# Four row buffers in place of five in a one-core MLA, sparse attention and PEER block, with reordered first loads and last stores

## The chip, the core and the metric

One core of a Trainium2 chip runs one launch. Its engines work in parallel from their own instruction queues and meet through semaphores: TensorE (PE in the profile, its weight loads PEld), VectorE (DVE), ScalarE (ACT), GpSimd (POOL) and SyncE (SP). DMAs are issued from the queues of SP, ACT and POOL. The metric is the device time of the launch in microseconds (us); the time before is the median of three runs.

## What is computed

A transformer layer for 256 tokens of width 2048 in float32: RMSNorm, an input projection (2048 x 4944), two groups of attention heads side by side, an output projection, a second RMSNorm, and a PEER layer with 16384 single-neuron experts. The part around the change is PEER:

```python
def peer(h, w_pq, sub_keys, u_tab, v_tab):
    def block(hb):
        b, t, _ = hb.shape
        qr = (hb @ w_pq).reshape(b, t, PEER_HEADS, 2, PEER_DKEY // 2)
        sc = jnp.einsum('bthpd,hpnd->bthpn', qr, sub_keys, preferred_element_type=jnp.float32)
        s_top, i_top = lax.top_k(sc, PEER_TOPK)
        cand = s_top[..., 0, :, None] + s_top[..., 1, None, :]
        c_top, c_pos = lax.top_k(cand.reshape(b, t, PEER_HEADS, PEER_TOPK * PEER_TOPK), PEER_TOPK)
        ...
        expert = i0 * PEER_NKEYS + i1
        g = jax.nn.softmax(c_top, axis=-1)
        u = u_tab[expert]
        a = jax.nn.gelu(jnp.einsum('bthkd,btd->bthk', u, hb, preferred_element_type=jnp.float32),
                        approximate=False)
        return jnp.einsum('bthk,bthkd->btd', (g * a).astype(v_tab.dtype), v_tab[expert])
```

Each token picks 8 x 16 = 128 experts. u_tab and v_tab are 134 MB each.

## The kernel before

**Two ways through PEER.** 96 of the 256 tokens ("own" tokens) go by gathers: for each of their picks the rows of u_tab and v_tab are fetched. The other 160 tokens (N_DN) go densely: all 128 units of u_tab (a unit is 128 experts, 1 MB) are multiplied by TensorE with the tokens' activations hF (the U pass, L1525), ScalarE applies GELU (L757), the result is multiplied by a gate matrix, and all 128 units of v_tab are multiplied with it (the V pass, L1580). Every fourth row of the first 128 tokens (`helpers`) lends its place to the picks of the others, so the picks of 96 tokens fill 96 gathers per table in 128 partitions. A gather brings one row of 2048 floats to each of the 128 partitions, 1 MB. There are 192, numbered n = 0 to 191: 96 of u_tab's rows, 96 of v_tab's.

**Row buffers.** Gathers go round through `row`, NROW buffers of 8 KB per partition; row[0] lies among the activations (`acts`), where before the gathers the gain row of the second norm is held, the others lie in `late`, the memory that the split weights and hidden state use until the last w_pq piece. A gather that reuses a buffer waits until VectorE has used it:

```python
                if n >= NROW:
                    pool.wait_ge(row_used, n + 1 - NROW)
                if n >= N_OWN:
                    pool.wait_ge(unit_used, PACE_FROM + (n - N_OWN) * (PACE_TO - PACE_FROM) // N_OWN)
```

The second wait paces V gathers by the units that TensorE has used. All gathers go through POOL's one queue. Ahead of every 16th u gather, POOL copies the lent picks of one head between partitions (`lend_picks`, L485 to L490), a small DMA on the same queue, and waits for it to land before it issues the next gather.

**VectorE** (next_row, L1134 to L1147) takes a u row (L1141: multiply with hs and sum, the dot product) or a v row (L1145: multiply with its weight and add to acc). While the top-k of PEER runs, it takes two rows after each head; in the late U pass it takes one row after each unit, except every 16th, behind its other work there, in program order: the one-hot matrices (hots, L1189) or the gate (L1203), then the multiply of a unit's GELU by ones or gates (apply, L1213), then the row.

**ScalarE** in the late U pass: GELU of unit c (needs the multiply of unit c - 2, whose buffer of two it reuses), in odd units the issue of the load of unit c + 4 (odd_unit, L777), and the scaling of the one-hot matrices for one gate group (hot_scale, L759 to L770). **TensorE** multiplies a unit, then in every second unit the gate group (L1542), which needs that scaling. The ring of units has four buffers; SP issues the even loads.

**Head.** The hidden state is split into a high and a low part as it is made: ScalarE norm_hi (L564, needs xT and the gains) and split_hi of weights (L544), VectorE norm_lo (L834) and split_lo (L821), then TensorE three matmuls for each piece. The first two k-slices of xT and the gains are issued by ScalarE, xT first; the first weight unit is one DMA of 512 KB from SP.

**Tail.** The last v unit closes the eight bank pairs of the output one after the other; ScalarE copies a pair out (L797), TensorE transposes it back (out_transposes, L1570), VectorE adds the residual (L1289), SP stores four groups of columns, two stores each (L426, L427).

## Time and profile before

| | |
|---|---|
| runs before, median (lowest to highest) | 1669.94 us (1669.61 to 1670.95) |
| the profiled execution: its time, its span | 1671.05 us, 1669.3 us |
| TensorE busy | 1656.0 us, 99% |
| VectorE, ScalarE, GpSimd busy | 1020.8, 504.0, 280.1 us |
| DMA, mean over the span; in the U and V passes | 341 GB/s; 392 to 422 GB/s in the page's slices 14 to 39 of 40 |

Busy time counts instructions of the engine, not the issue of DMAs. The page's chain of work that ended last runs for 85% of the span over TensorE and for 9% over DMAs; a DMA in it between about 875 and 1016 us is a gather or a copy of picks.

### The profile page before, as it was taken

The numbers are of one execution on the slowest core, as the hardware profiler recorded it, in microseconds if no ns is written. First come the engines' busy times: TensorE is split into PE (matmuls) and PEld (weight loads), VectorE is DVE, ScalarE is ACT, GpSimd is POOL, SyncE is SP. The second block draws the span as 40 slices with busy tenths as digits, with TensorE's granted clock in tenths as the row PEclk, the third lists the DMA queues.
The fourth block names the chain that finished last, engine by engine and source line by source line (L and its number), as shares of the span: only waits on it lengthen the run. The fifth ranks groups of instructions, "written<-read, shape, count | busy, mean of one in ns | idle before, by whom it ended". The sixth has DMA issues, their size and how long they took to land.

```text
span 1669.3 us, 28850 instructions
## 1 busy us (share of the span) xinstructions
PE 1656.0 (99%) x11438; PEld 1570.3 (94%) x11438; DVE 1020.8 (61%) x1709; ACT 504.0 (30%) x1347; POOL 280.1 (17%) x252
## 2 busy tenths in 40 slices
PE   9999999999999999999999999999999999999999
PEld 7768888888999999999999999999999999999998
DVE  5426695767778999867777767753444333433333
ACT  6547567656551000035444454410000000000000
POOL 1020000000003222312212122222112211221110
PEclk9999999999999999999999999999999999999999
DMA  9674445465648999999999999999999999999996
GB/s 355 226 149 125 139 135 193 139 225 201 224 159 334 421 397 419 411 392 420 395 422 420 421 401 422 422 421 421 421 421 417 417 415 421 422 417 419 421 415 237
DMA packets 107056, 569.90 MB, mean 341 GB/s; under 512 B 11280, under 2 KB 13456, under 8 KB 48208
## 3 DMA queue, kind: packets, MB, share of 16 engines
q1 hardware_dynamic: 56768, 216.22, 34.5%
q0 software_dynamic: 31792, 220.50, 32.9%
q10 hardware_dynamic: 18432, 132.41, 19.2%
q8 instruction: 29, 0.48, 0.1%
q14 instruction: 35, 0.29, 0.0%
HBM read 563.04 MB, written 4.46 MB: 340 GB/s over the span
## 4 chain that ended last, share of the span: by engine, by line
PE 85%; DMA 9%; DVE 2%; issue 1%; ACT 1%; POOL 1%; ACTq 0%; DVEq 0%
PE ps L1580 31%; PE ps L1525 25%; PE ps L1318 6%; PE ps L1320 5%; PE ps L1319 5%; DMA late<-in_u_rows,sel 4%; DMA sel<-sel 3%; DMA raw<-in_v_tab 2%; PE ps L1337 2%; PE ps L1474 2%; PE ps L1476 2%; PE ps L1475 2%; PE ps L1542 1%; DVE w_lo L821 1%; PE ps L1441 1%
## 5 line engine op out<-in xcount | busy, mean ns | idle before, releaser
L1145 DVE SCALAR_TENSOR_TENSOR acts<-late,sel,acts 128x2048 f32<-128x2048 f32 x77 | 181.1, 2352 | 248.6 <-DMA late<-in_v_tab,sel 248.3
L1525 PE MATMUL ps<-acts,late 128*128 128x160 f32 x2048 | 287.8, 300 | 0.0
L1525 PE MATMUL ps<-acts,raw 128*128 128x160 f32 x2048 | 287.6, 300 | 0.0
L1580 PE MATMUL ps<-acts,raw 128*128 (+1 forms) x2048 | 283.8, 299 | 1.0 <-DMA raw<-in_v_tab 0.7
L1580 PE MATMUL ps<-acts,late 128*128 (+1 forms) x2048 | 284.2, 299 | 0.0
L1580 PEld LDWEIGHTS ps<-acts,raw 128*128 128x128 f32 x2048 | 279.8, 190 | 1.9 <-issue 1.9
L1525 PEld LDWEIGHTS ps<-acts,late 128*128 128x128 f32 x2048 | 280.5, 190 | 0.0
L1525 PEld LDWEIGHTS ps<-acts,raw 128*128 128x128 f32 x2048 | 280.4, 190 | 0.0
L1580 PEld LDWEIGHTS ps<-acts,late 128*128 128x128 f32 x2048 | 280.1, 190 | 0.1
L821 DVE TENSOR_TENSOR w_lo<-raw,w_hi 128x512 fp32r<-128x512 f32 (+1 forms) x288 | 189.5, 683 | 132.8 <-ACT w_hi L544 130.6
L544 ACT ACTIVATE w_hi<-raw 128x512 fp32r<-128x512 f32 (+1 forms) x288 | 171.0, 622 | 89.0 <-PE ps L1320 42.8
L1141 DVE SCALAR_TENSOR_TENSOR late<-late,acts 128x2048 f32<-128x2048 f32 x76 | 173.3, 2289 | 39.9 <-DMA late<-in_u_rows,sel 39.7
L1318 PE MATMUL ps<-w_hi,hT_hi 128*128 128x512 f32 (+1 forms) x448 | 185.8, 415 | 5.2 <-DVE w_lo L821 5.1
L1320 PE MATMUL ps<-w_hi,hT_lo 128*128 128x512 f32 (+1 forms) x448 | 174.7, 390 | 0.0
L1319 PE MATMUL ps<-w_lo,hT_hi 128*128 128x512 f32 (+1 forms) x448 | 174.3, 389 | 0.0
L797 ACT ACTIVATE acts<-ps 128x320 f32<-128x320 f32 x8 | 3.5, 437 | 557.3 <-PE ps L1580 557.0
L483 POOL DMA_INDIRECT late<-in_v_tab,sel x77 | 90.9, 1180 | 374.8 <-PE ps L1580 238.2
L483 POOL DMA_INDIRECT late<-in_u_rows,sel x76 | 94.0, 1237 | 293.0 <-DVE late L1141 213.9
L1318 PEld LDWEIGHTS ps<-w_hi,hT_hi 128*128 128x128 f32 x448 | 84.9, 190 | 27.3 <-DVE w_lo L821 7.1
L1319 PEld LDWEIGHTS ps<-w_lo,hT_hi 128*128 128x128 f32 x448 | 85.1, 190 | 17.8 <-issue 3.1
L1320 PEld LDWEIGHTS ps<-w_hi,hT_lo 128*128 128x128 f32 x448 | 84.8, 189 | 17.3
L757 ACT ACTIVATE early<-ps 128x160 f32<-128x160 f32 x80 | 24.3, 303 | 200.4 <-PE ps L1525 180.0
(224 smaller groups left out, 1609.2 us busy)
## 6 DMA issues: line engine op xcount, KB each, us to landing
raw<-in_w_in SPq DMA_DIRECT2D x72, 512.0 KB, 3.5
raw<-in_u_tab SPq DMA_DIRECT2D x33, 1024.0 KB
late<-in_u_tab SPq DMA_DIRECT2D x33, 1024.0 KB
raw<-in_v_tab SPq DMA_DIRECT2D x32, 1024.0 KB
raw<-in_v_tab ACTq DMA_DIRECT2D x32, 1024.0 KB
late<-in_v_tab SPq DMA_DIRECT2D x32, 1024.0 KB
late<-in_v_tab ACTq DMA_DIRECT2D x32, 1024.0 KB
raw<-in_u_tab ACTq DMA_DIRECT2D x31, 1024.0 KB
```

What stands on the lines that cost most here:

```text
L483: pool.indirect_dma_start(row[n % NROW], None, table, bass.IndirectOffsetOnAxis(ap=idx[:, k:k + 1], axis=0)).then_inc(row_in[n % NROW], 16)
L544: nc.scalar.activation(whi[(2 * j + half) % NPART][:, 0:w], raw[j % NRAW][:, half * w:half * w + w], ACT.Copy).then_inc(hi_done, 1)
L821: V.tensor_tensor(wlo[slot_no][:, 0:w], raw[j % NRAW][:, half * w:half * w + w], whi[slot_no][:, 0:w].bitcast(F32), ALU.subtract).then_inc ...
L1141: V.scalar_tensor_tensor(row[n % NROW], row[n % NROW], 1.0, hs[turn % 2], ALU.mult, ALU.mult, accum_out=a_sel[:, n:n + 1]).then_inc(row_us ...
L1145: V.scalar_tensor_tensor(acc, row[n % NROW], w_sp[:, n - N_OWN:n - N_OWN + 1], acc, ALU.mult, ALU.add).then_inc(row_used, 1)
L1318: mm(out, hT_hi[:, k, t], whi[part][:, 0:w], start=start and kk == 0, stop=False)
L1319: mm(out, hT_hi[:, k, t], wlo[part][:, 0:w], start=False, stop=False)
L1320: ins = mm(out, hT_lo[:, k, t], whi[part][:, 0:w], start=False, stop=stop and kk == 1)
L1337: ins = mm(ps[:, bank, :], src[:, k, b * P:b * P + P], w[:, k, :], start=k == 0, stop=k == ks - 1)
L1474: mm(out, whi[piece % NPART][:, w], hT_hi[:, k, :], start=k == 0, stop=False)
L1525: ins = mm(ps[:, q, 0:N_DN], ring[q][:, k * P:k * P + P], hF[:, k, :], start=k == 0, stop=k == KD - 1)
L1580: ins = mm(ps[:, pair_bank(k // 2), at:at + N_DN], ring[q][:, k * P:k * P + P], acts[:, ds(i * (4 * N_DN) + q * N_DN, N_DN)], start=first ...
```

## The change

Four parts, two of which concern the row buffers' place, two the two ends of the launch.

1. NROW is 4. The four buffers are those in `late`; the region in `acts` keeps the gain row under a name of its own, gain_row, and is no longer a row buffer. The first gather therefore waits for the last w_pq piece (piece_used), as only the second did; the wait for hs in front of it goes, the same wait in front of the copies of hs stays. Counts in POOL's sequence that are written with NROW move by one or two gathers.
2. ScalarE issues the gains ahead of xT's first slices.
3. The first weight unit comes in two DMAs of 256 KB, one per k-slice; ScalarE splits the first half when the first has landed (first_in).
4. In the last v unit, a pair's transposes stand behind the first matmul of a later pair, not behind its second; and the stores of the helper rows are issued by ScalarE behind its last copy.

```diff
-    NRING, NROW = 4, 5
+    NRING, NROW = 4, 4
...
-        row = [region(A_ROW, D)] + [late[:, (2 + i) * D:(3 + i) * D] for i in range(4)]
+        gain_row = region(A_ROW, D)
+        row = [late[:, (2 + i) * D:(3 + i) * D] for i in range(4)]
...
             win = io["w_in"].rearrange("(k p) n -> p k n", p=P)
-            for n in range(8):
+            sp.dma_start(raw[0][:, 0:512], win[:, 0, 0:512]).then_inc(first_in, 16)
+            sp.dma_start(raw[0][:, 512:1024], win[:, 1, 0:512]).then_inc(raw_ready[0], 16)
+            for n in range(1, 8):
                 k = slice(2 * n, 2 * n + 2)
-                if n:
-                    sp.dma_start(xT[:, k, :], io["xT"][:, k, :]).then_inc(xT_in[n], 16)
+                sp.dma_start(xT[:, k, :], io["xT"][:, k, :]).then_inc(xT_in[n], 16)
                 load(n, n, win[:, k, 0:512])
...
                 sp.dma_start(io["out"][P:SEQ, cols], o_rest[0][:, cols]).then_inc(out_sent, 16)
-                sp.dma_start(io["out"][helpers, cols], o_rest[1][:, cols]).then_inc(out_sent, 16)
...
                 if n == 0:
-                    pool.wait_ge(hs_ready, 2)
-                if n == 1:
                     pool.wait_ge(piece_used, 2 * B_U)
...
-                act.wait_ge(raw_ready[j % NRAW], (u - j % NRAW) * (16 // NRAW) + 16)
+                first_unit = isinstance(u, int) and u == 0
+                act.wait_ge(first_in if first_unit else raw_ready[j % NRAW], (u - j % NRAW) * (16 // NRAW) + 16)
                 for half in range(2):
+                    if first_unit and half:
+                        act.wait_ge(raw_ready[0], 16)
...
+            act.dma_start(gains[:, :], io["gains"]).then_inc(gain_in, 16)
             act.dma_start(xT[:, 0:2, :], io["xT"][:, 0:2, :]).then_inc(xT_in[0], 16)
-            act.dma_start(gains[:, :], io["gains"]).then_inc(gain_in, 16)
...
+            for n in range(4):
+                act.wait_ge(out_ready, 4 * n + 4)
+                cols = slice(n * 512, n * 512 + 512)
+                act.dma_start(io["out"][helpers, cols], o_rest[1][:, cols]).then_inc(out_sent, 16)
...
                     if last and k % 2:
                         ins.then_inc(pair_mm, 1)
-                        if k >= 5:
-                            out_transposes(k // 2 - 2)
+                    elif last and k >= 4:
+                        out_transposes(k // 2 - 2)
```

POOL's queue where the gathers begin, before (acts and late tell a gather's buffer; hs goes by the two DMAs acts<-acts):

```order
L489 DMA sel<-sel 32x16 [waits idx_ready]
L483 DMA acts<-in_u_rows,sel 128x2048 [waits hs_ready,idx_in]
L502 DMA acts<-acts 32x2048 [waits hs_ready]
L502 DMA acts<-acts 32x2048
L483 DMA late<-in_u_rows,sel 128x2048 [waits piece_used]
L483 DMA late<-in_u_rows,sel 128x2048 x3
L505 MEMSET acts 128x8704 [waits score_done]
L483 DMA acts<-in_u_rows,sel 128x2048 [waits row_used]
L483 DMA late<-in_u_rows,sel 128x2048 [waits row_used] x4
```

and with the change:

```order
L488 DMA sel<-sel 32x16 [waits idx_ready]
L482 DMA late<-in_u_rows,sel 128x2048 [waits piece_used,idx_in]
L501 DMA acts<-acts 32x2048 [waits hs_ready]
L501 DMA acts<-acts 32x2048
L482 DMA late<-in_u_rows,sel 128x2048 x3
L504 MEMSET acts 128x8704 [waits score_done]
L482 DMA late<-in_u_rows,sel 128x2048 [waits row_used] x8
L507 MEMSET acts 128x2048 [waits slot_ready]
```

The first gather now goes to `late` and waits for piece_used; three gathers, not four, stand between the copies of hs and the memset, and every later gather waits for the row used four places earlier.

TensorE's queue at the end of the launch, before (L1580 are the v unit's matmuls, L1570 the transposes of one pair; the last rows):

```order
L1580 MATMUL ps<-acts,late 128x160 x2
L1570 MATMUL ps<-ident,acts 128x128 [waits outT_done]
L1570 MATMUL ps<-ident,acts 128x128
L1570 MATMUL ps<-ident,acts 32x128 x2
L1580 MATMUL ps<-acts,late 128x160 x2
L1570 MATMUL ps<-ident,acts 128x128 [waits outT_done]
L1570 MATMUL ps<-ident,acts 128x128
L1570 MATMUL ps<-ident,acts 32x128 x2
L1570 MATMUL ps<-ident,acts 128x128 [waits outT_done]
L1570 MATMUL ps<-ident,acts 128x128
L1570 MATMUL ps<-ident,acts 32x128 x2
```

and with the change (L1586 and L1576 are the same lines):

```order
L1586 MATMUL ps<-acts,late 128x160 x2
L1576 MATMUL ps<-ident,acts 128x128 [waits outT_done]
L1576 MATMUL ps<-ident,acts 128x128
L1576 MATMUL ps<-ident,acts 32x128 x2
L1586 MATMUL ps<-acts,late 128x160
L1576 MATMUL ps<-ident,acts 128x128 [waits outT_done]
L1576 MATMUL ps<-ident,acts 128x128
L1576 MATMUL ps<-ident,acts 32x128 x2
L1576 MATMUL ps<-ident,acts 128x128 [waits outT_done]
L1576 MATMUL ps<-ident,acts 128x128
L1576 MATMUL ps<-ident,acts 32x128 x2
```

The last matmul of the unit, which stood ahead of three pairs' transposes, now stands between those of the third-last pair and those of the last two.

## Rows read from the trace of the kernel before

**Rows 1.** the page: TensorE's busy time; its V-unit group, mean ns last
```profile
PE 1656.0 (99%) x11438; PEld 1570.3 (94%) x11438; DVE 1020.8 (61%) x1709; ACT 504.0 (30%) x1347; POOL 280.1 (17%) x252
...
L1580 PE MATMUL ps<-acts,late 128*128 (+1 forms) x2048 | 284.2, 299 | 0.0
```

**Rows 2.** TensorE's waits: engine line <- whom: us in total, times, longest
```profile
PE ps L1542 <- ACT acts L770: 1.1, 1, 1.1
```

**Rows 3.** windows: stretch, us; busy us (instructions) per engine, granted clock, DMA share, GB/s
```profile
905.00:985.00 80.00, 80.00 (x646) 78.83 (x646) 58.62 (x71) 36.91 (x120) 15.64 (x15) 1.00 1.01 418
```

**Rows 4.** timeline of ScalarE: start us, us, line, operation [idle before <- releaser]
```profile
997.68 0.30 ACT L757 ACTIVATE early<-ps 128x160 f32<-128x160 f32 x1 [4.37 <-PE ps L1525]
...
1007.17 0.30 ACT L757 ACTIVATE early<-ps 128x160 f32<-128x160 f32 x1 [4.83 <-PE ps L1525]
...
1017.88 0.30 ACT L757 ACTIVATE early<-ps 128x160 f32<-128x160 f32 x1 [4.92 <-DVE acts L1213]
```

**Rows 5.** timeline of VectorE in the U pass (rows L1141, multiplies L1213, gates L1203)
```profile
732.06 2.29 DVE L1141 SCALAR_TENSOR_TENSOR acts<-acts 128x2048 f32<-128x2048 f32 x1
...
888.96 1.17 DVE L1203 TENSOR_TENSOR acts<-acts,ps 128x512 f32<-128x512 f32 x1 [2.04 <-PE ps L1542]
...
991.48 2.29 DVE L1141 SCALAR_TENSOR_TENSOR acts<-acts 128x2048 f32<-128x2048 f32 x1 [3.84 <-DMA acts<-in_u_rows,sel]
...
994.94 0.31 DVE L1213 TENSOR_TENSOR acts<-acts,early 128x160 f32<-128x160 f32 x1
997.90 2.29 DVE L1141 SCALAR_TENSOR_TENSOR late<-late,acts 128x2048 f32<-128x2048 f32 x1 [2.64 <-DMA late<-in_u_rows,sel]
...
1003.17 2.29 DVE L1141 SCALAR_TENSOR_TENSOR late<-late,acts 128x2048 f32<-128x2048 f32 x1 [1.47 <-DMA late<-in_u_rows,sel]
...
1006.59 0.32 DVE L1213 TENSOR_TENSOR acts<-acts,early 128x160 f32<-128x160 f32 x1
...
1017.46 0.32 DVE L1213 TENSOR_TENSOR acts<-acts,early 128x160 f32<-128x160 f32 x1
```

**Rows 6.** timeline of GpSimd in the U pass: issues of gathers
```profile
734.63 0.93 POOL L483 DMA_INDIRECT acts<-in_u_rows,sel  x1 [11.38 <-DVE acts L1141]
...
984.71 2.24 POOL L483 DMA_INDIRECT acts<-in_u_rows,sel  x1 [22.09 <-DMA sel<-sel]
```

**Rows 7.** timeline of GpSimd in the V pass
```profile
1597.20 0.94 POOL L483 DMA_INDIRECT late<-in_v_tab,sel  x1 [3.41 <-PE ps L1580]
```

**Rows 8.** timeline of VectorE in the V pass
```profile
1587.09 2.35 DVE L1145 SCALAR_TENSOR_TENSOR acts<-late,sel,acts 128x2048 f32<-128x2048 f32 x1 [3.24 <-DMA late<-in_v_tab,sel]
```

**Rows 9.** chain that ended last, in the head: start us, us, what
```profile
1.21 4.49 DMA gains<-in_gains
```

**Rows 10.** timeline of all engines, head
```profile
0.76 0.42 ACTq L615 DMA_DIRECT2D acts<-in_xT  x1
...
5.72 0.91 ACT L564 ACTIVATE hT_hi<-acts,gains 128x256 fp32r<-128x256 f32 x2 [2.54 <-DMA gains<-in_gains]
...
8.02 0.77 PE L1318 MATMUL ps<-w_hi,hT_hi 128*128 128x512 f32 x1 [2.15 <-DVE w_lo L821]
...
13.28 0.63 PE L1318 MATMUL ps<-w_hi,hT_hi 128*128 128x512 f32 x1
...
14.37 0.39 PE L1318 MATMUL ps<-w_hi,hT_hi 128*128 128x512 f32 x1
```

**Rows 11.** DMA issues: count, KB each, median us to landing
```profile
acts<-in_xT ACTq DMA_DIRECT2D x1, 256.0 KB, 3.6
```

**Rows 12.** windows, columns as in rows 3, head
```profile
8.00:14.00 6.00, 5.98 (x14) 4.74 (x15) 3.96 (x8) 3.54 (x8) 2.37 (x5) 1.00 1.05 401
```

**Rows 13.** timeline of all engines, tail
```profile
1664.30 2.07 DVE L1289 TENSOR_TENSOR acts<-ps,acts 128x256 f32<-128x256 f32 x6 [0.24 <-PE ps L1570]
...
1666.39 0.33 SPq L426 DMA_DIRECT2D out<-acts  x1
1666.77 0.43 SPq L427 DMA_DIRECT2D out<-acts  x1
```

More of the change, by code:

```diff
@@ L247, in build_block @@
         hs_in, idx_in, gsp_in, mask_set, acc_set, turn_kept = sem("hs_in"), sem("idx_in"), sem("gsp_in"), sem("mask_set"), sem("acc_set"), sem("turn_kept")
-        lent_in, acc_sum, warm_set = sem("lent_in"), sem("acc_sum"), sem("warm_set")
+        lent_in, acc_sum, warm_set, first_in = sem("lent_in"), sem("acc_sum"), sem("warm_set"), sem("first_in")
         gsp_ready, a_done, w_ready, acc_in = sem("gsp_ready"), sem("a_done"), sem("w_ready"), sem("acc_in")
@@ L465, in _ @@
             pool.dma_start(subk, io["sub_keys"]).then_inc(subk_in, 16)
-            pool.dma_start(row[0], io["g_row"].to_broadcast([P, D])).then_inc(gain_row_in, 16)
+            pool.dma_start(gain_row, io["g_row"].to_broadcast([P, D])).then_inc(gain_row_in, 16)
             pool.wait_ge(x2_done, 16)
@@ L1169, in _ @@
             for i in range(2):
-                V.scalar_tensor_tensor(hs[i], x2[0], rs_x[:, 0:1], row[0], ALU.mult, ALU.mult).then_inc(hs_ready, 1)
+                V.scalar_tensor_tensor(hs[i], x2[0], rs_x[:, 0:1], gain_row, ALU.mult, ALU.mult).then_inc(hs_ready, 1)
             V.tensor_reduce(help_count, ident[:, helpers], AX, ALU.add).then_inc(mask_set, 1)
```

## The prediction

> **What bounds the kernel now.** I read the page's busy times first: TensorE works for 1656.0 of the 1669.3 us of the span [rows 1], so a cost counts only where TensorE itself stands, and a gain only where TensorE starts earlier or the end comes sooner after its last instruction. Then TensorE's waits: there are few. Outside the head the one that bears on the row buffers is a single 1.1 us at L1542, the gate matmuls, for ScalarE [rows 2]. I followed it back. ScalarE was late because its GELU of an odd unit waited for VectorE's multiply L1213, and VectorE was late because it stood at L1141 for gathered rows. In that stretch the DMA engines are full: 418 GB/s at a share of 1.01 [rows 3]. Two streams share them. TensorE takes two units of 1 MB each in 9.49 us (997.68 to 1007.17 [rows 4]), which is 2 x 1.049 / 9.49 = 221 GB/s; 197 GB/s are left for the gathers, and 1.049 MB at that rate take 5.3 us. VectorE's rows say the same: with a wait for the DMA ahead of each, it takes rows at 997.90 and 1003.17, 5.27 us apart [rows 5]. So late in the U pass the gather queue is a server with 5.27 us a row, and it is just too slow for VectorE, which by its program wants one row per unit (4.74 us) in 15 units of 16.
>
> **The change, part by part.** *Four row buffers, start.* The first gather now goes into memory that the last weights still use, so it waits for the last weight piece instead of for hs; both come at the end of the weights, and the queue behind it holds the same four gathers. During the top-k work VectorE takes two rows and then a whole head's top-k without any; nothing there uses up five buffers. I price both at 0.
>
> *Four row buffers, the late U pass.* At 732.06 VectorE uses row 30 [rows 5], which frees a buffer, and POOL issues the next gather at 734.63 [rows 6]. With five buffers that is the gather of row 35, since 31 to 34 lie in the other four; with four it is the gather of row 34. From there to the next copy of picks the queue has work without a gap in both kernels, so each later row lands one service later: 5.27 us. A queue that serves one row at a time does not get slower by having fewer rows in it, as long as it never runs dry: from the start of its use to the end of its next issue a buffer is away for 3.5 us (732.06 to 735.56), and if landing and start add as much again, the other three still hold 3 x 5.27 = 15.8 us of service. So the loss is a single row's time, once, not one per row. At 888.96 it hides: VectorE still waits 2.04 us for TensorE ahead of each gate [rows 5].
>
> Where does it come to the surface? The GELU of an odd unit c needs the multiply L1213 of unit c-2. In the three odd units before and at TensorE's wait, the multiplies end at 994.94 + 0.31 = 995.25, 1006.91 and 1017.78 [rows 5], and the GELUs start at 997.68, 1007.17 and 1017.88 [rows 4]: 2.4 us spare, then 0.3, then none, and this last is the 1.1 us. All of ScalarE's scaling, and so the gate matmuls, follow that GELU directly. With every row 5.27 us later, the first of the three is late by 5.27 - 2.4 = 2.9 us, and if nothing is given back the three together cost 5.27 us more than the 1.1 of now. Give-back: while TensorE stands, no units are fetched, and their 221 GB/s go to the gathers; a stall of x us moves the gathers ahead by 221/197 x = 1.1x, so if all of it came in time the cost would be 5.27 / 2.1 = 2.5 us. Between these ends I take **+4.2 us**, nearer the upper, because the lateness arrives in one step: after the copy of picks the POOL has stood 22.09 us and the queue has run empty [rows 6], VectorE waits 3.84 and 2.64 us for the next two rows [rows 5], and the stall follows within one unit; what it gives back reaches only the rows behind it.
>
> *The V pass.* POOL is paced there by the units that TensorE has used. The gather at 1597.20 [rows 7] is four rows behind the one that VectorE uses at 1587.09 [rows 8]; that row's buffer is free at 1587.09 + 2.35 = 1589.44, 7.8 us before the issue. Four buffers cost 0. The first few V rows come later by a place, and nothing on TensorE waits for them.
>
> *Head.* ScalarE's first norm step starts at 5.72, when the gains land: issued second on ScalarE's queue at 1.21, 4.49 us on the way [rows 9, 10]. The 256 KB of xT, issued first at 0.76 [rows 10], take 3.6 us [rows 11], to 4.36. Exchanged, the gains go ahead and xT, issued 0.45 us later, lands at about 4.8: 0.9 us sooner. The first weight unit is fetched in halves of 256 KB, so its first half is there by about the same time, under the 0.91 us of the two norm steps [rows 10]; without that cover ScalarE would wait for it. SP issues one more DMA, which puts the seven xT pieces and units behind it off by about 0.45 us; TensorE needs the second unit only 12 matmuls after the first, which covers that. TensorE's first matmul at 8.02 moves to about 7.1. What that is worth depends on the matmuls' rate: at 13.28 they still last 0.63 us, at 14.37 they last 0.39 [rows 10]. If the faster rate comes no sooner, 0.9 x 0.39 / 0.63 = 0.5 us is kept; if it moves along, 0.9. I take **-0.75 us**; the rest of the kernel follows TensorE.
>
> From 8 to 14 us the granted clock reads 1.00, its upper level of 2.4 GHz [rows 12], after TensorE has stood 2.15 us before its first weight matmul, so the trace doesn't name the clock as the cause of the two durations. The Trainium skill ("TensorE: Matmul & The Clock Gate", Part 1: The HAM clock gate) says that the array is held back by default, at 1.2 instead of 2.4 GHz, and that activity releases it, after a number of slow matmuls that varies from run to run; by that, the head's gain could be well above mine in one run and below it in another.
>
> *Tail.* The last transposes stand one matmul earlier, 2 x 284.2 / 2048 = 0.28 us [rows 1]. VectorE's last six additions run without a gap from 1664.30 for 2.07 us [rows 13], so they may start 0.28 us earlier; the last pair's transposes now follow the last matmul closely and wait some 0.3 us for ScalarE's copy, which takes a third of that back. The two last stores were issued one behind the other by SP, at 1666.39 and 1666.77 [rows 13]; now ScalarE issues the second, after three others of its own (0.43 us each, as at 1666.77) behind its last copy, about as late as VectorE's last addition. At most 0.28 + 0.38 = 0.66 us is saved, at least nothing; I take **-0.25 us**, since the larger store of the two ends at almost the same time as the smaller one.
>
> The Trainium skill ("DMA: Bandwidth & Descriptors", Issuing engines are not separate DMA queues) speaks against more: DMAs issued from several engines run on the same 16 engines and interleave, so only issue time is saved. The trace agrees with it, since the two streams of the U pass add up to one 418 GB/s.
>
> **Sum.** +4.2 - 0.75 - 0.25 = +3.2 us. The profiled execution took 1671.05 us, so its own successor would take 1674.25; that execution lies 1.1 us above the median of the runs, 1669.94, and I carry the difference over: **1673.1 us**. 0.2%, about what a measurement of this kernel can tell from no change, is 3.3 us, so the forecast is a small loss at the edge of what can be seen.
>
> **The rivals.** *Slower, plainly.* After a copy of picks the queue starts empty, and VectorE lives on what lies in its buffers: one row fewer. If it runs dry at the restart, it pays the rest of the restart too: the first row's wait of 3.84 us there less the usual 1.47 [rows 5] is 2.4 us. With nothing given back that is 5.27 to 7.7, less 0.5 and 0.25 a net of +4.5 to +6.9, some 1675.5 us. It decides once TensorE's waits for ScalarE in the U pass exceed 5.5 us. For it: the 22.09 us. Against: the queue's work is the same, and one such step is already in my sum.
>
> *Given back.* The stall spreads over units and the units' bandwidth reaches the gathers in time: +2.5 - 1.0 = +1.5, 1671.4 us. For it: the 418 GB/s are a sum that stays. Against: the single step.
>
> *Hidden.* VectorE's lateness stays under ScalarE's spare time: only head and tail are left, -1.0, 1668.9 us. For it: 2.04 us of waiting at 888.96. Against: the last spare is 0 already [rows 4, 5].
>
> *Faster.* Hidden, and the head's slow matmuls end sooner: they last from 8.02 to beyond 13.28, and at the faster rate 5.3 x (1 - 0.39 / 0.63) = 2.0 us of that would go; -1.0 - 2.0 = -3.0 and, with the larger tail gain, -3.4, about 1666.5 us. It needs two things at once, and no row here shows the second. What the Trainium skill says of the varying number of slow matmuls ("TensorE: Matmul & The Clock Gate", Part 1) would allow it.
>
> **How the numbers follow.** My forecast 0.45, slower plainly 0.20, given back 0.17, hidden 0.11, faster 0.07. The forecast's own range is +2.3 to +4.5 us; about half of it lies above 3.3. Slower by over 0.2%: 0.20 and half of 0.45, some 0.42. Faster by over 0.2%: most of the last, 0.06. Within: 0.52. The range goes from "hidden" (1668.8) to the upper part of "slower plainly" (1675.8), and leaves out some 0.15.
>
> **What would show it.** In the changed kernel's profile: TensorE's waits for ScalarE at the gate matmuls grow from 1.1 to about 5 us, most of it in one place soon after 985 us; VectorE waits for rows of u_rows sooner; rows land 5.2 to 5.3 us apart as before; the first matmul stands near 7.1 us; the last addition ends about 0.2 us earlier relative to the last matmul. I am wrong if rows land further apart with four buffers (then depth sets the rate, and the loss is per row), if TensorE waits for V rows' work, or if the first matmul does not move.

## The result and the profile after

The changed kernel took **1676.71 us** (median of 7 runs, 1674.67 to 1679.05) against 1669.97 (1669.54 to 1670.95) for the kernel before, run beside it: a ratio of 1.0035, interval 1.0022 to 1.0047, which is **+3.7 to +7.8 us**. The forecast was 1673.1 us with a range up to 1675.8: the side is right, the loss is about twice the forecast, and above the range. The profiled execution of the changed kernel is the slowest of its seven, 1679.05 us with a span of 1677.3; the times spread over 4.4 us where those of before spread over 1.4 (in the later studies the kernel before spreads over 3.5 to 6.9).

TensorE is busy for 1.0 us more than before (first line of the page, as in [rows 1]) in a span that is 8.0 us longer: most of the difference is waiting.

```profile
PE 1657.0 (99%) x11438; PEld 1570.5 (94%) x11438; DVE 1020.2 (61%) x1709; ACT 503.8 (30%) x1347; POOL 281.5 (17%) x252
```

TensorE's waits (line <- whom: us in total, times, longest). L1548 is L1542 of [rows 2], L1586 the V units, L1324 the projections' first matmuls:

```profile
PE ps L1324 <- DVE w_lo L827: 8.5, 7, 3.0
...
PE ps L1548 <- ACT acts L772: 2.0, 1, 2.0
PE ps L1586 <- DMA raw<-in_v_tab: 1.9, 3, 1.0
PE ps L1548 <- ACT early L772: 1.8, 2, 1.2
```

At the gate matmuls 3.8 us in three waits, for the 1.1 us of [rows 2]; at the V table 1.9 us (0.7 before); in the head one wait of 3 us that the kernel before does not have. The three waits at the gate, from TensorE's timeline:

```profile
940.59 0.84 PE L1548 MATMUL ps<-early 128*128 128x128 bf16 x12 [1.16 <-ACT early L772]
...
960.45 0.84 PE L1548 MATMUL ps<-early 128*128 128x128 bf16 x12 [0.65 <-ACT early L772]
...
1009.96 0.84 PE L1548 MATMUL ps<-acts 128*128 128x128 bf16 x12 [1.98 <-ACT acts L772]
```

GpSimd's restarts after the copies of picks, to hold against 984.71 of [rows 6], and VectorE's rows round the second of them (as [rows 5]):

```profile
907.65 2.22 POOL L482 DMA_INDIRECT late<-in_u_rows,sel  x1 [17.73 <-DMA sel<-sel]
...
994.23 2.25 POOL L482 DMA_INDIRECT late<-in_u_rows,sel  x1 [17.28 <-DMA sel<-sel]
```

```profile
988.07 2.29 DVE L1147 SCALAR_TENSOR_TENSOR late<-late,acts 128x2048 f32<-128x2048 f32 x1 [1.46 <-DMA late<-in_u_rows,sel]
...
993.35 2.29 DVE L1147 SCALAR_TENSOR_TENSOR late<-late,acts 128x2048 f32<-128x2048 f32 x1 [1.54 <-DMA late<-in_u_rows,sel]
...
1001.90 2.29 DVE L1147 SCALAR_TENSOR_TENSOR late<-late,acts 128x2048 f32<-128x2048 f32 x1 [4.73 <-DMA late<-in_u_rows,sel]
```

Rows come 5.28 us apart, as forecast, until the copy; across the restart two rows are 8.55 us apart (7.66 in the kernel before, from 983.82 to the 991.48 of [rows 5]). Each of the two late restarts is followed by waits of TensorE, the first by two, the second by one.

The head. The chain of work, from the start to the end of the unforeseen wait, then windows over it (granted clock, DMA share and GB/s are the last three numbers):

```profile
1.21 4.49 DMA acts<-in_xT
5.79 0.91 ACT hT_hi L566 x2
...
8.09 0.49 PE ps L1324
...
11.57 0.40 PE ps L1326
11.97 0.24 PE ps L1324
...
16.81 13.65 DMA raw<-in_w_in
30.49 0.64 ACT w_hi L546
31.15 0.70 DVE w_lo L827
31.99 0.50 PE ps L1324
```

```profile
30.00:32.00 2.00, 0.01 (x1) 0.04 (x1) 0.85 (x2) 1.51 (x3) 0.00 (x0) 1.00 1.02 385
32.00:34.00 2.00, 2.00 (x6) 1.58 (x7) 1.46 (x3) 1.93 (x6) 0.00 (x0) 0.57 1.04 414
34.00:36.00 2.00, 2.00 (x7) 1.59 (x6) 0.90 (x2) 0.72 (x2) 0.00 (x0) 0.57 0.98 332
36.00:38.00 2.00, 2.00 (x7) 0.70 (x6) 0.82 (x3) 1.24 (x3) 0.00 (x0) 1.00 0.65 248
```

Second on its queue, xT lands as late as the gains did in [rows 9], and the first matmul does not move (8.02 in [rows 10]). In this chain the matmuls come 0.23 us apart from 11.97 on, in that of the kernel before from 14.29; TensorE then stands 2.96 us for the weights of the eighth unit, 13.65 us on their way, and the granted clock behind it lies near the lower level for 4 us. The first matmul behind the next wait, the same instruction in both kernels, sums the head up; it is 3.67 us later (65.79 against 62.12; the second line is the kernel before):

```profile
65.79 0.50 PE L1324 MATMUL ps<-w_hi,hT_hi 128*128 128x512 f32 x1 [0.84 <-DVE w_lo L827]
```

```profile
62.12 0.50 PE L1318 MATMUL ps<-w_hi,hT_hi 128*128 128x512 f32 x1 [0.84 <-DVE w_lo L821]
```

In the tail, ScalarE's four stores are issued by 1674.44 and VectorE's additions end at 1674.05 (1666.37 in [rows 13]):

```profile
1671.85 2.20 DVE L1295 TENSOR_TENSOR acts<-ps,acts 128x256 f32<-128x256 f32 x6 [0.24 <-PE ps L1576]
...
1672.13 2.31 ACTq L804 DMA_DIRECT2D out<-acts  x4
```

From ScalarE's first copy of the tail to the end of the span it is 11.6 us, 11.4 before: 0.2 us more.

Four places, then, in this execution: head +3.7, U pass +2.7, V pass +1.2, tail +0.2, together 7.8 of the 8.0 us between the two profiled executions.

### The profile page after: what moved, and what is told of

It reads as the page before. It is cut to its first block, busy times and chain, and to the rows that moved or that the text cites. A ratio compares the mean times of both kernels' runs of the same rounds, so it can differ in the third digit from the quotient of the medians.

```text
span 1677.3 us, 28851 instructions
## 1 busy us (share of the span) xinstructions
PE 1657.0 (99%) x11438; PEld 1570.5 (94%) x11438; DVE 1020.2 (61%) x1709; ACT 503.8 (30%) x1347; POOL 281.5 (17%) x252
## 4 chain that ended last, share of the span: by engine, by line
PE 81%; DMA 13%; DVE 2%; issue 2%; ACT 1%; POOL 1%; ACTq 0%; DVEq 0%
PE ps L1586 31%; PE ps L1531 22%; DMA late<-in_u_rows,sel 7%; PE ps L1324 5%; PE ps L1326 5%; PE ps L1325 5%; DMA sel<-sel 3%; DMA raw<-in_v_tab 2%; PE ps L1343 2%; PE ps L1480 2%; PE ps L1482 2%; PE ps L1481 2%; PE ps L1548 1%; DMA raw<-in_w_in 1%; DVE w_lo L827 1%
## 5 line engine op out<-in xcount | busy, mean ns | idle before, releaser
L1151 DVE SCALAR_TENSOR_TENSOR acts<-late,sel,acts 128x2048 f32<-128x2048 f32 x96 | 225.7, 2351 | 314.9 <-DMA late<-in_v_tab,sel 314.6
L1586 PE MATMUL ps<-acts,raw 128*128 (+1 forms) x2048 | 283.8, 299 | 2.0 <-DMA raw<-in_v_tab 1.9
L1586 PE MATMUL ps<-acts,late 128*128 (+1 forms) x2048 | 284.4, 299 | 0.0
L1586 PEld LDWEIGHTS ps<-acts,raw 128*128 128x128 f32 x2048 | 279.8, 190 | 2.9 <-issue 2.9
L1586 PEld LDWEIGHTS ps<-acts,late 128*128 128x128 f32 x2048 | 280.1, 190 | 0.1
L1147 DVE SCALAR_TENSOR_TENSOR late<-late,acts 128x2048 f32<-128x2048 f32 x96 | 218.7, 2290 | 73.9 <-DMA late<-in_u_rows,sel 70.8
L482 POOL DMA_INDIRECT late<-in_v_tab,sel x96 | 119.7, 1247 | 455.3 <-PE ps L1586 312.1
L1324 PE MATMUL ps<-w_hi,hT_hi 128*128 128x512 f32 (+1 forms) x448 | 185.8, 415 | 8.6 <-DVE w_lo L827 8.5
L482 POOL DMA_INDIRECT late<-in_u_rows,sel x96 | 120.7, 1257 | 399.4 <-DVE late L1147 299.9
L1324 PEld LDWEIGHTS ps<-w_hi,hT_hi 128*128 128x128 f32 x448 | 85.2, 190 | 31.0 <-issue 7.2
```

The lines of the kernel that those rows point to most:

```text
L482: pool.indirect_dma_start(row[n % NROW], None, table, bass.IndirectOffsetOnAxis(ap=idx[:, k:k + 1], axis=0)).then_inc(row_in[n % NROW], 16)
L1147: V.scalar_tensor_tensor(row[n % NROW], row[n % NROW], 1.0, hs[turn % 2], ALU.mult, ALU.mult, accum_out=a_sel[:, n:n + 1]).then_inc(row_us ...
L1151: V.scalar_tensor_tensor(acc, row[n % NROW], w_sp[:, n - N_OWN:n - N_OWN + 1], acc, ALU.mult, ALU.add).then_inc(row_used, 1)
L1324: mm(out, hT_hi[:, k, t], whi[part][:, 0:w], start=start and kk == 0, stop=False)
L1586: ins = mm(ps[:, pair_bank(k // 2), at:at + N_DN], ring[q][:, k * P:k * P + P], acts[:, ds(i * (4 * N_DN) + q * N_DN, N_DN)], start=first ...
```

## The experiments

My theory after these two profiles was that the four prices are separate; the rival, that the four buffers cost nearly all and the head was chance. Each kernel below is the kernel before, or the changed one where said, with the edit shown.

**Each part alone.** Four buffers are the hunks on NROW, `row`, `gain_row` and the first gather's wait. The shorter head is the order of the two loads on ScalarE's queue and the first unit in halves. The shorter tail is the stores' queue and the earlier transposes. The cores of the three edits:

```diff
-    NRING, NROW = 4, 5
+    NRING, NROW = 4, 4
```

> The kernel before with four row buffers and nothing else of the change. Theory A (three separate prices, read from the two profiles of before and after: head +3.7, late U pass +2.7, V pass +1.2, tail +0.4): the time is 2.5 to 4 us over the kernel before (about 1673.5), TensorE waits at the gate matmuls for some 3 to 4 us in all (1.1 before), nearly all of it within 60 us of the two restarts of the gather queue (near 900 and 985), and the first units of the input projection are as in the kernel before, with no wait after the first matmul of 8.0 us. Rival B (the four buffers cost nearly everything, and the stall in the head of the changed kernel was chance): +5.5 to +7, waits at the gate matmuls and at the V table for 5 us or more together. Rival C (the buffers cost nothing, all of it is the head and tail): within 1 us of before.

Ratio 1.0022 (1.0012 to 1.0032), +2.0 to +5.3 us. Theory A's time lies in this interval, those of B and C outside. TensorE's waits:

```profile
PE ps L1541 <- ACT acts L769: 2.1, 1, 2.1
PE ps L1541 <- ACT early L769: 1.7, 2, 1.1
```

The three waits stand at 935.80, 955.68 and 1005.29, at the places of the changed kernel. Behind the last one there is something that the first profile did not have:

```profile
1004.00:1006.00 2.00, 0.71 (x13) 0.71 (x13) 1.90 (x3) 1.54 (x5) 0.94 (x1) 1.00 1.06 451
1006.00:1008.00 2.00, 2.00 (x11) 2.00 (x9) 2.00 (x3) 0.00 (x0) 0.00 (x0) 0.50 0.97 410
1008.00:1010.00 2.00, 2.00 (x11) 2.00 (x10) 0.95 (x3) 0.00 (x0) 1.33 (x1) 0.65 1.04 438
1010.00:1012.00 2.00, 2.00 (x17) 2.00 (x16) 1.11 (x1) 0.00 (x0) 0.00 (x0) 1.00 0.98 410
```

```profile
1005.29 0.85 PE L1541 MATMUL ps<-acts 128*128 128x128 bf16 x12 [2.07 <-ACT acts L769]
1005.97 6.24 PE L1524 MATMUL ps<-acts,late 128*128 128x160 f32 x32
1012.04 4.51 PE L1524 MATMUL ps<-acts,raw 128*128 128x160 f32 x32
```

The granted clock falls to 0.50, its lower level of 1.2 GHz, and 32 matmuls take 6.24 instead of 4.51 us: a wait of 2.07 us costs 1.7 us more than itself.

```diff
+            act.dma_start(gains[:, :], io["gains"]).then_inc(gain_in, 16)
             act.dma_start(xT[:, 0:2, :], io["xT"][:, 0:2, :]).then_inc(xT_in[0], 16)
-            act.dma_start(gains[:, :], io["gains"]).then_inc(gain_in, 16)
```

> The kernel before with the shorter head alone: the gains before xT on the queue of ScalarE, the first weights in two transfers. Theory A: 2.5 to 3.7 us slower than before (about 1673); the matmuls of the input projection come 0.23 us apart from about 12 us on instead of 14 us, TensorE runs into weights that have not landed and stands 2 to 3 us near 30 us, and then starts matmuls 0.43 us apart for some 3 us more; where an execution does not do that, it is about 1 us faster than before, so the runs spread by several us. Rival B: within 1 us of before, and the profile shows no wait of TensorE between 9 and 60 us. Rival D (the head as it was forecast): 0.5 to 0.9 us faster.

Ratio 1.0007 (0.9998 to 1.0016), -0.3 to +2.7 us: neither gain nor loss is told apart. Theory A's loss of 2.5 to 3.7 us is at the edge of this, the forecast's gain of 0.5 to 0.9 outside. The first matmul stands at 7.71, and near 29 us TensorE waits, briefly:

```profile
28.97 0.47 PE L1322 MATMUL ps<-w_hi,hT_hi 128*128 128x512 f32 x1 [0.33 <-DVE w_lo L825]
```

```diff
-                        if k >= 5:
-                            out_transposes(k // 2 - 2)
+                    elif last and k >= 4:
+                        out_transposes(k // 2 - 2)
```

> The kernel before with the shorter tail alone: the stores of the lent rows on the queue of ScalarE, the transposes two matmuls earlier. Theory A: within 0.5 us of before, and from the last matmul of the V pass to the end of the span as long as before within 0.4 us. Rival (the transposes that now stand between the last matmuls of the V pass delay these, and ScalarE's queue lands its store later): 0.5 to 1 us slower. Rival (as it was forecast): 0.25 to 0.66 us faster.

Ratio 0.9999 (0.9990 to 1.0008), and no gain in its profile: ScalarE's first copy of the tail to the end is 11.6 us, 11.4 before.

In its head, which the tail's edit does not touch, the matmuls come 0.23 us apart at the start and again from 12.65 us on, and the matmul near 61 us stands at 60.87, 1.25 us ahead of the kernel before:

```profile
60.87 0.50 PE L1321 MATMUL ps<-w_hi,hT_hi 128*128 128x512 f32 x1 [0.85 <-DVE w_lo L824]
```

So when the rate rises is not set by the shorter head: of the eleven profiles without that edit eight show the early rise (0.23 us apart for good by 13 us), three the late one (not before 13.5); of the nine with it, seven and two.

**The restart.** Is it the shift by a row that costs, or the empty queue at the copies of picks? The copy for rows 48, 64 and 80 is put into the queue eight rows ahead, and only its landing is waited for where it stood:

```diff
-                    if n < N_OWN and n % TOPK == 0:
-                        lend_picks(n // TOPK)
+                    h = n // TOPK
+                    if n < N_OWN and n % TOPK == 0:
+                        if h < 3:
+                            lend_picks(h)
+                        pool.wait_ge(idx_in, 16 * (h + 1))
+                    if n % TOPK == 8 and 3 <= h + 1 < N_OWN // TOPK:
+                        lend_picks(h + 1)
```

> Four row buffers as in the first of these runs, and the copies of the picks for rows 48, 64 and 80 put into the queue eight rows earlier, so that the gather queue does not run empty at them. Theory E (the price of the fourth buffer in the U pass is paid at the restarts, where VectorE finds no row and falls behind ScalarE's next units): the rows from 700 to 1060 us come without a gap of over 12 us, the waits at the gate matmuls fall to 1 us or less, and the time is 2 to 4 us under that of four buffers alone. Rival F (it is the rate of the gathers, one row each 5.2 us against one unit each 4.74 us, that puts VectorE behind, whatever the restarts do): the waits at the gate matmuls stay at 3 us or more, only at another place, and the time stays within 1 us of four buffers alone.

Ratio 0.9999 (0.9990 to 1.0009) with four buffers: the loss is gone, -4.2 us between the two medians. GpSimd's groups from 700 to 1060 us (busy, mean ns | idle before), first with four buffers alone, then with the early copies:

```profile
L482 POOL DMA_INDIRECT late<-in_u_rows,sel x67 | 74.0, 1104 | 277.9 <-DVE late L1140 206.5 <-DMA sel<-sel 67.4 <-issue 4.0
```

```profile
L482 POOL DMA_INDIRECT late<-in_u_rows,sel x66 | 69.8, 1058 | 278.9 <-DVE late L1144 254.1 <-DMA sel<-sel 23.6 <-issue 1.2
```

Of 67.4 us of standing for copies, 23.6 are left (the copy for row 32, which was not moved), and TensorE's wait at the gate is 0.3 us in all. The rate of the gathers alone, one row each 5.3 us, makes TensorE wait for no more than these 0.3 us, even with four buffers.

**The changed kernel again, and less volume in its head.**

> The changed kernel itself once more, beside the kernels below on the same chip, with a new profile. By the parts so far (four buffers +3.7, head +1.2, tail about 0, each with some 1.5 us of uncertainty) it is 3.5 to 6.5 us slower than before. Theory A' (the gate waits of the U pass are the same 3.8 us in every execution; the stall of TensorE near 30 us with the slow stretch behind it comes in some executions only): the new profile shows the gate waits again, at 3 to 4 us, and a stall near 30 us that is anything between 0 and 3 us; the time differs between executions by that. Rival (the head of the changed kernel always stalls as in its first profile): again 2 to 3 us of wait near 30 us and starts 0.43 us apart behind it.

Ratio 1.0037 (1.0023 to 1.0051). The profiled execution took 1680.43 us; the gate waits are 5.8 us and not the same 3.8 that theory A' expected, the longest is followed by a slow stretch again, and in the head TensorE stands 1.60 us:

```profile
30.74 0.47 PE L1324 MATMUL ps<-w_hi,hT_hi 128*128 128x512 f32 x1 [1.60 <-DVE w_lo L827]
...
1009.25 1.46 PE L1548 MATMUL ps<-acts 128*128 128x128 bf16 x12 [3.62 <-ACT acts L772]
```

The next edit relieves the DMA engines, which are full in the head ([rows 12], and 385 to 414 GB/s above):

```diff
-                pool.wait_ge(piece_used, 10 + 4 * i)
+                pool.wait_ge(piece_used, 18 + 3 * i)
```

> The kernel before with one edit in the head that is not of the change: the six transfers of the up-projections' weights, 768 or 1024 KB each, wait for weight pieces 18, 21, 24, 27, 30, 33 in place of 10, 14, 18, 22, 26, 30, so that two of them no longer run beside the first weights. Theory G (the DMA engines are the bound of the first 32 us once TensorE's matmuls come 0.23 us apart early, which they do in some executions of every kernel): weights and xT land earlier, ScalarE's waits for weights of 1 to 2.4 us near 26 and 30 us are gone, and the time is 0 to 1.5 us under before, with fewer executions at its slow end. Rival (the head has slack, the DMA engines only look full): within 0.5 us of before either way, the same spread, ScalarE waits as before.

> The shorter head alone, together with the later transfers of the up-projections' weights. Theory G: what cost the shorter head its gain is the room on the DMA engines between 12 and 31 us; with 1.5 MB moved out of it TensorE does not stop after its first matmul near 7.7 us until the projection's end, and the kernel is 0.3 to 1.5 us faster than before and 1 to 3 us faster than the shorter head alone. Rival (the order of the first transfers is what delays the weights of unit 7, not the volume): TensorE stops near 29 us as with the shorter head alone, and the time is the shorter head's, 0 to 2.5 us over before.

Ratios 1.0002 (0.9993 to 1.0011) and 1.0005 (0.9996 to 1.0014): no effect on the time that these runs can tell, and no stop of TensorE in either head. Both profiles fell on the late rise, in which the kernel before does not stop either, so they do not separate volume from order.

**Three buffers** (`NROW = 3`, one buffer out of the list):

> The kernel before with three row buffers, one less again than the change has. Theory A: a buffer less moves VectorE's rows behind a restart of the gather queue by one row's service of 5.3 us; from five to four some 2 us of that fell into slack, from four to three nothing does, so the waits at the gate matmuls are 7 to 10 us in all (3.8 with four, 1.1 with five), and the time is some 8 to 10 us over before. Rival H (both restarts pay the whole shift, and the queue of three runs empty between rows too): waits of over 13 us, 14 us or more over before. Rival I (the price grows by the same 3 us from step to step): waits near 6.5 us, some 6.5 us over before.

Ratio 1.0045 (1.0030 to 1.0060), +5.0 to +10.0 us; the gate waits are 9.3 us:

```profile
PE ps L1541 <- ACT acts L769: 7.2, 4, 4.7
...
PE ps L1541 <- ACT early L769: 2.1, 2, 1.6
```

By the waits theory A holds: 9.3 us lies in its 7 to 10, and the step from four to three adds about 5 us to the mean of the profiles with four, near one row's service. The interval of the time does not exclude rival I's 6.5 us. The profiled execution is the slowest of its four, and the 4.7 us wait, at 933.89, is again followed by a slow stretch.

**Undoing and repairing the changed kernel.** With the old head; with the relief; and the early copies on the kernel before and, with the relief, on the changed kernel:

> The changed kernel with its head undone: four row buffers and the shorter tail, the first loads as in the kernel before. If the head change is what the changed kernel has beyond the price of its four buffers (two profiles showed TensorE standing 2.96 and 1.60 us near 30 us, which none of the six profiles without both edits did for more than 0.33 us), this is 3 to 4.5 us over before, 2 to 3 us under the changed kernel, with no wait of TensorE between 9 and 60 us. Rival (buffers and tail together cost all of it, the stall is noise of the head): 6 to 7 us over before, as the changed kernel.

> The changed kernel with the later transfers of the up-projections' weights (weight pieces 18, 21, 24, 27, 30, 33 in place of 10 to 30 by fours). Theory G (volume on the DMA engines from 16 to 31 us makes the stall): 1.5 to 3 us under the changed kernel, about 4 us over before, and no wait of TensorE over 0.5 us between 9 and 60 us. Rival (the stall comes from what bunches earlier, the masks and x behind the late first matmuls, before these weights are issued at 24 us): the stall stays at 1 us or more, and the time is the changed kernel's within 1 us.

> The kernel before, five row buffers, with the copies of the picks for rows 48, 64 and 80 put into the queue eight rows earlier. Theory E (restarts are what makes TensorE wait in the U pass): the waits at the gate matmuls, 1.1 us before, are 0 to 0.4 us, the time is 0.3 to 1.2 us under before, the most that this can bring. Rival (with the rows earlier the gathers take DMA time from the tables, and TensorE waits for these instead): waits for the V table of 1.5 us or more, the time within 0.5 us of before or above it.

> The changed kernel with both repairs: the copies of the picks eight rows earlier, and the later transfers of the up-projections' weights. If the two causes are the restarts of the gather queue and the crowded DMA engines of the head, nearly all of the loss is gone: within 1.5 us of before, gate waits of 0.5 us or less, no stall near 30 us. If only the first is right, it is 1.5 to 3.5 us over before.

Old head: 1.0032 (1.0021 to 1.0043), 0.5 to 1.8 us under the three ratios of the changed kernel and within their intervals, with no stop in the head; that is less than expected of the head. Relief: 1.0036 (1.0022 to 1.0049), no better than the changed kernel, although its profile shows no stop in the head; the expected 1.5 to 3 us are not there. Early copies on the kernel before: **0.9989 (0.9980 to 0.9998), 1668.72 us**, no gate wait at all, and the runs spread over 1.8 us (those of before beside it over 4.1). Early copies and relief on the changed kernel: 1.0002 (0.9993 to 1.0011), as the expectation for both causes has it, though with 1.3 us of gate waits where it had 0.5 or less. Since the relief alone showed no gain, the 5.6 us between its median and this one are put down to the early copies; on the changed kernel these were not tried without the relief.

**Head and tail without the noise of the U pass**, on top of the early copies, five buffers:

> The kernel before with the copies of the picks eight rows earlier, once more, as what the next three are measured against: 1 to 2.5 us under before, over a spread of some 2 us, no wait of TensorE at the gate matmuls of more than 0.5 us and no stretch with a lower granted clock between 700 and 1650 us.

> Early copies of the picks and the shorter head. Theory G (the DMA engines are full from 8 to 31 us, so an earlier start only brings TensorE sooner to weights that have not landed): the median is 0.5 to 2 us over the copies alone, and some executions lie 3 to 5 us over, those in which a stop near 30 us is followed by a slow stretch of matmuls. Rival (in most executions the earlier start stays): 0.2 to 0.5 us under the copies alone, by the first matmul at 7.7 to 7.8 us in place of 8.0. Rival (forecast): 0.5 to 0.9 us under.

> Early copies of the picks, the shorter head and the later transfers of the up-projections' weights. Theory G: the stop near 30 us is gone (it was in two profiles with four buffers), so the median is 0 to 0.5 us under the copies alone and no execution lies 3 us over it. Rival (volume is not the reason): as with copies and head, or the same as the copies alone in every respect but 0.3 us.

> Early copies of the picks and the shorter tail. By the profiles the last addition ends 0.14 us earlier after the first copy of the tail, and the end of the span comes 0.2 us later, since the last stores take longer to land: 0.2 us over the copies alone. Rival (forecast): 0.25 us under. Both are at the limit of what 5 rounds tell.

Copies alone 0.9994 (0.9985 to 1.0003), with the head 0.9993, with head and relief 0.9991, with the tail 0.9988, each interval 0.0009 to either side. Medians 1668.67, 1668.72, 1668.99 and 1669.20. With five buffers and the early copies, then, neither head nor tail nor relief shows a gain or a loss: the medians lie within 0.6 us of each other, less than these intervals tell. The profile with the relief stops TensorE for 0.52 us near 29 us, so volume is not the whole reason of that stop. With the head, the matmuls of the seventh unit run 0.2 us ahead of the copies alone (at 26 us) and those of the eighth 0.2 us behind (at 31 us): what the start gains goes again at the weights of the eighth unit. In the fifteen profiles with the early rise these weights are issued at 16.7 to 17.1 us with the old head and land at 25.7 to 27.3; with the new one they are issued at 16.5 to 16.8 and land at 27.0 to 30.5: issued as early, they land later, by what path is not shown.

**Four buffers and the whole change, side by side:**

> Four row buffers alone, once more. Theory K (the loss is the waits of the late U pass, 2 to 5 us, and in some executions a stretch at half rate behind the longest of them, 1.7 to 2.7 us, beside 0.7 us at the V table; head and tail add 0 to 0.5): 4 to 6 us over before, and within 1.5 us of the whole change. Rival L (with four buffers the head loses too): 2.5 to 4 us over before, 2 to 3 us under the whole change.

> The whole change, once more. Theory K: 4.5 to 6.5 us over before, within 1.5 us of the four buffers alone; the profile shows waits at the gate matmuls of 2 to 6 us, and where one is over 2 us perhaps a granted clock of 0.5 behind it. Rival L: 6 to 7.5 us over before, with TensorE standing 1.5 us or more near 30 us.

Ratios 1.0035 (1.0022 to 1.0048) and 1.0043 (1.0031 to 1.0055), medians 1676.13 and 1678.14 beside 1670.49. Theory K fits the first median (+5.6); the second (+7.7 by the medians, +7.2 by the ratio) lies 1.2 or 0.7 us above its 6.5. Rival L fits the second time by the ratio, but without the stop that it needs, and lies under the first. The intervals overlap. Four buffers alone make most of the loss, not all of it: over all studies, against the kernel before in the same study, the 23 executions with four buffers and the new head (the changed kernel in three studies, and with the relief) lie 6.6 us higher on the mean, the 21 with four buffers and the old head (four buffers alone in two studies, and the changed kernel with the old head) 4.6. Only two pairs of these ran side by side, 2.0 and 0.7 us apart by their means. The profile of the whole change has no stop in the head at all, and gate waits of 5.5 us with a slow stretch behind the longest, in which 32 matmuls take 6.95 us:

```profile
1007.50 1.46 PE L1548 MATMUL ps<-acts 128*128 128x128 bf16 x12 [3.40 <-ACT acts L772]
1008.76 6.95 PE L1531 MATMUL ps<-acts,late 128*128 128x160 f32 x32
1015.54 4.51 PE L1531 MATMUL ps<-acts,raw 128*128 128x160 f32 x32
```

**The account.** For single executions the times can be put together from rows: gate waits, waits at the V table, the extra time of the slow stretch in the U pass (the gate's 12 and the next 32 matmuls over 0.84 and 4.51 us) and where the matmul near 61 us stands. The sum is of the differences to the kernel before; the tail is left out.

| execution | time | gate waits | V waits | slow stretch | near 61 us | sum | measured |
|---|---|---|---|---|---|---|---|
| before | 1671.05 | 1.1 | 0.7 | 0 | 62.12 | | |
| changed, first | 1679.05 | 3.8 | 1.9 | 0 | 65.79 | +7.6 | +8.0 |
| changed, second | 1680.43 | 5.8 | 1.3 | 2.8 | 62.97 | +9.0 | +9.4 |
| changed, third | 1679.13 | 5.5 | 1.3 | 3.1 | 61.79 | +7.8 | +8.1 |
| four buffers, first | 1675.11 | 3.8 | 1.1 | 1.7 | 60.88 | +3.6 | +4.1 |
| four buffers, second | 1674.85 | 5.1 | 1.4 | 0 | 61.17 | +3.8 | +3.8 |
| changed, old head | 1672.52 | 2.2 | 1.2 | 0 | 60.94 | +0.4 | +1.5 |
| changed, relief | 1674.05 | 4.2 | 1.6 | 0 | 60.89 | +2.8 | +3.0 |
| changed, both repairs | 1671.63 | 1.3 | 1.6 | 0 | 60.95 | -0.1 | +0.6 |
| tail alone | 1668.45 | 0 | 0.4 | 0 | 60.87 | -2.7 | -2.6 |
| early copies | 1668.10 | 0 | 0.5 | 0 | 60.95 | -2.5 | -3.0 |
| three buffers | 1682.78 | 9.3 | 1.9 | 1.7 | 61.23 | +10.2 | +11.7 |

These columns explain the executions to within 0.7 us, but for two (1.1 and 1.5 us are left); the eight profiles that are not in the table come out within 0.9. The large entries that move with the number of buffers are the gate waits and what follows them.

## Why the prediction was wrong in size

Three terms of the sum failed: the gains of 1.0 us at head and tail, which did not come; the 0 for the V pass, which is +0.7 us; and the late U pass, which had no price for the clock behind a wait, 1.1 us on the mean of seven profiles and 2.0 in the three of the changed kernel.

*The late U pass, +4.2 us.* The mechanism stands: one buffer less, rows 5.28 us apart, VectorE late, ScalarE late, TensorE waiting at the gate. The size of the waits themselves was fair: 3.8, 5.8 and 5.5 us in the three profiles of the changed kernel against 1.1, so +2.7 to +4.7 and on the mean +3.9. What I had not priced is the clock behind a wait. In two of the three profiles the longest wait was followed by a granted clock of 0.50 and 2.8 and 3.1 us of extra time, on the mean 2.0. With this consequence the term is some +6 us in these three. They lie 1.0 to 3.7 us above the medians of their studies; over the seven profiles with four buffers and the copies where they stood, the waits grow by 3.2 and the slow stretch takes 1.1, together +4.3, as much as I forecast without it.

*"Most of it in one place soon after 985".* Wrong: both late restarts surface. The waits at 940 and 960 follow the restart at 907, and the hidden reserve that I read at 888.96 [rows 5] did not outlast it.

*"A queue that serves one row at a time does not get slower by having fewer rows in it, as long as it never runs dry".* True as a sentence, and the condition fails at each copy of picks. The early copies show it: with the queue kept filled, four buffers take what five take without it (0.9999), against 0.9989 for five with it (the intervals overlap); of the 1.7 us between these, 0.8 us are waits at the V table and 0.3 at the gate in the two profiles. The fifth buffer was VectorE's reserve across the copies.

*"Slower, plainly"* came nearest: it was to decide once the waits exceed 5.5 us, and they were 3.8, 5.8 and 5.5. I gave it 0.20 because I had put one restart into my sum already. Its time, 1675.5, is still 1.2 us low: it lacked the clock too, and it counted the head and the tail as gains.

*V pass, 0.* Wrong by a little. The waits at the V table are 1.1 to 1.9 us in all nine profiles with four buffers and 0.4 to 0.9 in all ten with five: some +0.7 us. I looked at GpSimd's pacing and not at what the transfers of the tables lose; by what path fewer buffers lengthen these waits was not tried.

*Head, -0.75.* The failed step is "xT, issued 0.45 us later, lands at about 4.8". It lands at 5.3 to 5.7. I had carried over the 3.6 us that it took as the first on its queue [rows 11]; as the second it takes 4.1 to 4.5, and in all profiles the second of the two, whichever it is, lands at 5.3 to 6.0. With the gains ahead the first matmul stands at 7.7 to 8.1 us in the profiles with the new head, against 7.9 to 8.35, so that it does not move, which I had named as a sign of being wrong. I also took the two rates from durations, 0.63 and 0.39 us, which overlap; the matmuls start 0.43 and 0.23 us apart. What little is gained goes again near 30 us. That side was not in my rivals. In the first profile the loss there is 3.7 us, in four of the nine profiles with the new head TensorE stops near 30 us (2.96, 1.60, 0.52, 0.33 us), in none of the eleven without it. The medians, though, show neither gain nor loss of the head on top of the early copies. What it adds with four buffers stays open: 0.5 to 1.8 us by the kernel with the old head put back, 2.0 us on the mean over all studies, in place of the -0.75. Why the weights of the eighth unit land late stays open too: less volume beside them did not settle it. With a head of 0 and the 0.7 us at the V table, the waits and the clock of all seven profiles come to +5.0 us, and up to +7 with that open part; measured were +6.7, +6.9 and +7.7 by the medians.

*Tail, -0.25.* The last addition does end sooner after ScalarE's first copy (8.37 us in the changed kernel, 8.51 before), half of what I expected, but from the first copy to the end of the span it is 0.2 us longer; the runs do not tell the tail from nothing.

*The start and the top-k part*, priced at 0, show no new wait.

## What to carry to other kernels

Buffers between an in-order queue and its consumer are priced at the points where the queue is made to run empty, not by its steady rate; look for the small transfers that are waited for in the middle of it, and issue them ahead. A wait of TensorE can have a second price behind it: behind five of the eight waits of 2.07 us and more that are listed below the granted clock was at its lower level for some microseconds. Put that into the bound as a case of its own. A gain in a stretch whose DMA engines are full has to be followed to the next transfer that is waited for, before it is booked.

## What the runs showed of the hardware

Leaving out the wait ahead of the first weight matmul, waits of TensorE of 2.07, 2.96, 3.40, 3.62 and 4.70 us were followed by a granted clock at or near 0.50, its lower level, and 1.7 to 3.1 us of extra time; waits of 1.98, 2.24, 2.28 and 2.76 us were not. So a wait of 2 to 3 us cost nearly double in some executions and not in others. The Trainium skill ("TensorE: Matmul & The Clock Gate", Part 1: The HAM clock gate) says that the array is throttled when it has been idle and that the window behind this runs free of the kernel; that the two lists overlap, 2.07 in one and 2.76 in the other, agrees with a window that runs free.

From 8 to 14 us of the kernel before the granted clock reads 1.00 [rows 12] while matmuls start 0.43 us apart; in the changed kernel the same spacing reads near 0.57 (8 to 12 and 32 to 36 us). At the very start of a trace the spacing of the matmuls is the safer reading.

When the rate rises in the head differs between executions of kernels whose heads are the same; for the matmul near 61 us it is 62.12 against 60.87, 1.25 us that no edit made.

The version with five buffers and the early copies has the lowest medians here, 1668.72 and 1668.67 us in its two studies. Its ratios to the kernel before are 0.9989 (0.9980 to 0.9998) and 0.9994 (0.9985 to 1.0003), 1.0 to 1.8 us; the second interval includes no change, so this is at the edge of what can be told.
